# Twenty-two gate groups instead of sixteen, x parked in DRAM, and two linear layers without GpSimd

## The reference

```python
s = jnp.einsum('blhtd,htnd->blhtn', q, sub_keys)
s1, i1 = lax.top_k(s[..., 0, :], 16);  s2, i2 = lax.top_k(s[..., 1, :], 16)
cand = s1[..., :, None] + s2[..., None, :]          # 16 best of 256 a head
...
act = jax.nn.gelu(jnp.einsum('td,tkd->tk', hx, u_tab[ix]))
return jnp.einsum('tk,tkd->td', gx * act, v_tab[ix])
```

## Time and profile before

| what | value |
|---|---|
| runs | 3215.37, 3218.54, 3218.54 us, median 3218.54 us |
| the profiled execution, its own time | 3217.91 us |
| its span, first to last instruction | 3216.1 us |
| mean granted TensorE clock | 0.964 of full speed |
| busy: PE, DVE, ACT, POOL | 2968.4, 2030.7, 1256.4, 155.5 us |

### The profile page before, as it was taken

One profiled execution on the slowest core, in us unless ns is written; L12 is line 12 of the kernel. 1 busy time (PEld: TensorE's weight loads), 2 busy tenths in 40 slices (PEclk: granted clock), 3 DMA queues, 4 the chain that ended last, 5 costly groups with the idle time before them and its releaser, 6 DMA issues. The chain is left out here.

```text
span 3216.1 us, 48665 instructions
## 1 busy us (share of the span) xinstructions
PE 2968.4 (92%) x17528; PEld 2670.5 (83%) x17528; DVE 2030.7 (63%) x3988; ACT 1256.4 (39%) x1826; POOL 155.5 (5%) x116
## 2 busy tenths in 40 slices
PE   7967797899999999999898888978999999999997
PEld 4946697789999999988687787977899999999885
DVE  8867679953348888878735645899534433443454
ACT  3343344753333333333342234458433333333333
POOL 0000350000000000000000012500000000000000
PEclk9988899999999999999988988999999999999999
DMA  5712233574457767767613232336644444444463
GB/s 207 275 39 102 85 118 122 220 246 155 154 183 246 240 237 236 248 193 229 203 46 121 78 119 79 118 125 236 235 153 145 151 155 153 144 152 155 138 176 109
DMA packets 324479, 524.86 MB, mean 163 GB/s; under 512 B 215536, under 2 KB 218352, under 8 KB 319872
## 3 DMA queue, kind: packets, MB, share of 16 engines
q1 hardware_dynamic: 321472, 472.89, 45.4%
q10 hardware_dynamic: 2880, 50.33, 3.9%
HBM read 449.00 MB, written 74.15 MB: 163 GB/s over the span
## 5 line engine op out<-in xcount | busy, mean ns | idle before, releaser
L1952 PE MATMUL pe_s<-peer_hi,pq_uh 128*128 128x384 f32 x2304 | 784.8, 341 | 23.4 <-DVE peer_lo L163 12.6
L163 DVE TENSOR_TENSOR val_vl<-val_vr,val_vh 128x1024 fp32r<-128x1024 f32 x256 | 313.7, 1225 | 757.8 <-ACT val_vh L2115 757.8
L1954 PE MATMUL pe_s<-peer_hi,pq_ul 128*128 128x384 f32 x2304 | 775.9, 337 | 0.0
L1953 PE MATMUL pe_s<-peer_lo,pq_uh 128*128 128x384 f32 x2304 | 775.7, 337 | 0.0
L2052 ACT ACTIVATE pe_A<-pe_s 128x384 f32 (+1 forms) x256 | 126.1, 493 | 1127.2 <-PE pe_s L1954 1127.2
L2019 PE MATMUL peer_acc<-val_vh,val_wh 128*128 128x512 f32 x1536 | 473.2, 389 | 1.0 <-DVE val_wl L163 1.0
L2019 PE MATMUL peer_acc<-val_vh,val_wl 128*128 128x512 f32 x1536 | 474.1, 390 | 0.0
L2019 PE MATMUL peer_acc<-val_vl,val_wh 128*128 128x512 f32 x1536 | 472.9, 389 | 0.0
L1952 PEld LDWEIGHTS pe_s<-peer_hi,pq_uh 128*128 128x128 f32 x2304 | 436.4, 189 | 43.5 <-issue 17.2
L1953 PEld LDWEIGHTS pe_s<-peer_lo,pq_uh 128*128 128x128 f32 x2304 | 436.9, 190 | 8.4
L1954 PEld LDWEIGHTS pe_s<-peer_hi,pq_ul 128*128 128x128 f32 x2304 | 436.4, 189 | 0.0
(11 more groups left out here) (458 smaller groups left out, 3519.6 us busy)
## 6 DMA issues: line engine op xcount, KB each, us to landing
pq_ur<-in_peer_u SPq DMA_DIRECT2D x256, 512.0 KB, 3.7
val_vr<-in_peer_v SPq DMA_DIRECT2D x256, 512.0 KB, 4.5
val_gr<-gates SPq DMA_DIRECT2D x256, 192.0 KB, 4.6
val_mrow<-in_ada_rows SPq DMA_DIRECT2D x56, 512.0 KB, 4.3
gates<-gate_stg ACTq DMA_DIRECT2D x6, 4096.0 KB, 12.5
pq_ur<-in_w_query SPq DMA_DIRECT2D x32, 512.0 KB, 3.6
s_wv<-val_out SPq DMA_DIRECT2D x32, 512.0 KB, 5.2
gates<-gate_stg ACTq DMA_DIRECT2D x4, 3072.0 KB, 13.0
```

The costliest lines, as they stand in the source:

```text
L163: return nc.vector.tensor_tensor(r32(out), x, hi, ALU.subtract)
L1952: pe.matmul(o, r32(uh[:, b, k]), r32(hi[:, k]), start=k == 0, stop=False)
L1953: pe.matmul(o, r32(uh[:, b, k]), r32(lo[:, k]), start=False, stop=False)
L1954: mm = pe.matmul(o, r32(ul[:, b, k]), r32(hi[:, k]), start=False, stop=k == KC - 1)
```

## The change

**Gate groups.** 22 groups of two chunks and a score block, four of them (2, 8, 14 and 20) with three chunks. `LAST` becomes 40, `RING` 44. The order in a group stays: DVE puts `table_low` behind the second chunk, PE runs the score block behind the group's chunks.

**Room.** The ring `A` grows by six blocks. For that, `i1`, `i2`, `gh`, `gl` and `eq` move to the place of `x`. SP stores x (1.57 MB) to DRAM in the query stage and loads it again behind the table, value and gate loads that stand before the slots.

**Rows and builds.** Two of the 24 early rows move from `mix_output` to the end of `mix_input`. In layer 0's slots, rows 0 to 49 stand in slots 34 to 83 as before, and the last six take two slots each (84 to 95), one product in each. Three builds stand in each of slots 34 to 63, two in each of 64 to 83, none in 84 to 95, and two in each of 96 to 126.

**Linear layers.** `Ahead.add` and `Ahead.low_part` go from GpSimd to DVE in both linear layers.

```diff
-IN_ROWS, OUT_ROWS = 2 * KC, KC
+IN_ROWS, OUT_ROWS = 2 * KC + 2, KC - 2
...
+                for i in range(WITH, IN_ROWS):
+                    rows.products(dve, i)
...
-    def low_part(self, pool, b):
-        pool.wait_ge(self.high, b + 1)
-        self.nc.gpsimd.tensor_tensor(r32(self.ul[:, b]), self.ur[:, b], self.uh[:, b], ALU.subtract).then_inc(self.low, 1)
+    def low_part(self, dve, b):
+        dve.wait_ge(self.high, b + 1)
+        lo_part(self.nc, self.ul[:, b], self.ur[:, b], self.uh[:, b]).then_inc(self.low, 1)
...
-        self.nc.gpsimd.tensor_tensor(self.sum[:], a, sq[:, k % self.RING], ALU.add).then_inc(self.added, 1)
+        self.nc.vector.tensor_tensor(self.sum[:], a, sq[:, k % self.RING], ALU.add).then_inc(self.added, 1)
...
-                    rows.products(dve, i)
+                    if i < OUT_ROWS:
+                        rows.products(dve, i)
+                    if i >= 3:
+                        ahead.add(dve, i - 2, sq)
+                    if 4 <= i < 6:
+                        ahead.low_part(dve, i - 4)
...
-GROUP = 3
+GROUPS = [3 if g % 6 == 2 else 2 for g in range(22)]
+SPANS = [range(sum(GROUPS[:g]), sum(GROUPS[:g + 1])) for g in range(22)]
...
-LAST = GATED + CHUNKS // GROUP
+LAST = GATED + len(SPANS)
...
-    THREES, TWOS, LAST_SLOT = ROWS_FROM, ROWS_FROM + 6, ROWS_FROM + 6 + (24 * KC - 18) // 2
+    STARTS = ((0, ROWS_FROM, 3), (90, ROWS_FROM + 30, 2), (130, ROWS_HALF + 12, 2))
...
+            sp.wait_ge(nm.ready, KC)
+            sp.dma_start(d["x_kept"], cx.x[:]).then_inc(xkept, 16)
...
+            sp.wait_ge(gated, CHUNKS)
+            sp.dma_start(cx.x[:], d["x_kept"]).then_inc(xback, 16)
...
-                for u in range(GROUP):
-                    gates((n - GATED) * GROUP + u)
+                for c in SPANS[n - GATED]:
+                    gates(c)
                 late(n)
...
-            for c in range(CHUNKS):
-                one_hots(c)
-                if c % GROUP == 1:
-                    n = GATED + c // GROUP
-                    table_low(n, n % 2)
+            for n in range(GATED, LAST):
+                for c in SPANS[n - GATED]:
+                    one_hots(c)
+                    if c == SPANS[n - GATED][1]:
+                        table_low(n, n % 2)
```

More of the change, by code:

```diff
@@ L689, in mix_input @@
     NY, NV = 18, 8
-    N = NY + NV
+    N, WITH = NY + NV, 2 * KC
     with Stage(nc, sems, "in0") as s:
@@ L729, in _ @@
                         sp.dma_start(d["s5_tab"], tab.all).then_inc(tab.stored, 16)
-                    if i >= N - IN_ROWS + 2:
-                        rows.load(sp, i - (N - IN_ROWS))
+                    if i >= N - WITH + 2:
+                        rows.load(sp, i - (N - WITH))
+                for i in range(WITH, IN_ROWS):
+                    rows.load(sp, i)
                 sp.wait_ge(rstored, 16)
@@ L833, in _ @@
                         dve.sem_inc(chain.made, 1)
-                    if i >= N - IN_ROWS:
-                        rows.products(dve, i - (N - IN_ROWS))
+                    if i >= N - WITH:
+                        rows.products(dve, i - (N - WITH))
+                for i in range(WITH, IN_ROWS):
+                    rows.products(dve, i)
 class Ahead:
@@ L1003, in _ @@
                     square(i)
[L1005 to L1010, removed]
 def scan_output(nc, sems, cx, d, scanned, hi, lo, fin, ahead):
@@ L1067, in _ @@
                         pair(i // 2 - 2)
+                    if i >= 7 and i % 2 == 1:
+                        ahead.add(dve, (i - 5) // 2, sq)
+                    if 9 <= i < 11:
+                        ahead.low_part(dve, i - 9)
                 pair(KC - 2)
+                ahead.add(dve, KC - 2, sq)
                 pair(KC - 1)
@@ L1115, in _ @@
                     ahead.square(act, k, cx.x[:, k], sq)
[L1117 to L1122, removed]
 def rope(nc, sems, cx, d, y, cache):
@@ L1671, with row_slot @@
 ROWS_AHEAD = 2
-ROWS_FROM = 34
+ROWS_FROM, ROWS_HALF = 34, 84
+def row_slot(row):
+    whole = ROWS_HALF - ROWS_FROM
+    return ROWS_FROM + row if row < whole else ROWS_HALF + 2 * (row - whole)
 GATED = FIRST + HOLD
-LAST = GATED + CHUNKS // GROUP
+LAST = GATED + len(SPANS)
 RING = LAST + TAIL
@@ L1740, in slot_of @@
     def slot_of(self, op):
-        return self.THREES + op // 3 if op < 18 else self.TWOS + (op - 18) // 2
+        first, slot, each = [x for x in self.STARTS if x[0] <= op][-1]
+        return slot + (op - first) // each
     def load(self, sp, q):
@@ L1824, in mix_experts @@
     ss = acc[:, 2, 0:T]
-    i1d, i2d, ghd, gld = (s.sb(x, [P, T, 2], F16) for x in ("i1", "i2", "gh", "gl"))
+    (i1d, i2d, ghd, gld), eq = cx.chosen, cx.equal
     warm = s.sb("warm", [P, 1])
@@ L1841, in mix_experts @@
         stg = x.sb("stg", [P, 2, NKEYS, HALF])
-        o1, eq, oh, ol = (x.sb(k, [P, 2, CT, P], F16) for k in ("o1", "eq", "oh", "ol"))
+        o1, oh, ol = (x.sb(k, [P, 2, CT, P], F16) for k in ("o1", "oh", "ol"))
     with Stage(nc, s.sems, f"val{layer}") as x:
@@ L1925, in slot @@
                         sp.dma_start(normg[:], d["norm_g"][:, 2:4]).then_inc(late_loaded, 16)
-                    row = z.n + ROWS_AHEAD - ROWS_FROM
-                    if 0 <= row < LATE_MODS:
+                    for row in (r for r in range(LATE_MODS) if row_slot(r) - ROWS_AHEAD == z.n):
                         if row >= ROWS_AHEAD:
@@ L1933, in _ @@
             slots(sp, slot, looped=layer > 0)
+            sp.wait_ge(xback, 16)
             if layer == 0:
@@ L2356, in _, with modulate @@
             table_low(RING, RING % 2)
-            def modulate(row):
+            def modulate(row, cs):
                 dve.wait_ge(row_loaded[row % ROWS_AHEAD], row // ROWS_AHEAD * 16 + 16)
@@ L2364, in modulate @@
                     dve.wait_ge(silu_loaded, 16)
-                for c, out in ((0, spare[:]), (1, mrow[:, row % ROWS_AHEAD])):
+                for c in cs:
+                    out = mrow[:, row % ROWS_AHEAD] if c else spare[:]
                     ins = v.scalar_tensor_tensor(out, mrow[:, row % ROWS_AHEAD], 1.0, silu[:, c], ALU.mult, ALU.mult,
                                                  accum_out=cx.modT[:, 2 * MODS - LATE_MODS + row, c:c + 1])
-                ins.then_inc(row_used, 1)
+                if c:
+                    ins.then_inc(row_used, 1)
             def modulated():
@@ L2385, in slot @@
                     apply(z, 1)
[L2386 to L2389, removed]
+                    if layer == 0:
+                        for row in range(LATE_MODS):
+                            if z.n < ROWS_HALF and row_slot(row) == z.n:
+                                modulate(row, (0, 1))
+                            elif row_slot(row) >= ROWS_HALF and row_slot(row) in (z.n, z.n - 1):
+                                modulate(row, (z.n - row_slot(row),))
+                        if z.n == row_slot(LATE_MODS - 1) + 2:
+                            modulated()
                     if layer == 0:
@@ L2912, in build @@
     sems = Semaphores(nc)
+    cx = Context()
+    with Stage(nc, sems, "gates") as g:
+        cx.chosen = [g.sb(x, [P, T, 2], F16) for x in ("i1", "i2", "gh", "gl")]
+        cx.equal = g.sb("eq", [P, 2, CT, P], F16)
     with Stage(nc, sems, "g") as g:
-        cx = Context()
-        cx.const, cx.x = g.sb("const", [P, C_KEEP]), g.sb("x", [P, KC, T])
+        cx.x, cx.const = g.sb("x", [P, KC, T]), g.sb("const", [P, C_KEEP])
         cx.modT, cx.scale = g.sb("modT", [P, 2 * MODS, 2]), g.sb("scale", [P, 2, 2, KC, 2])
```

14 lines of the change are left out of this document (10 added, 4 removed).

## The result

The changed kernel takes 3197.72 us (median, 3195.92 to 3201.61), the kernel before, beside it, 3218.54 us. The ratio is 0.9939, 95% interval 0.9923 to 0.9956: faster by 20.8 us, a little under half of the 42.3 forecast. The time lies inside the range given (3160 to 3200), but above the likeliest case's own range, at the time of the second rival (3198).

A forecast was written before the change was run, and what follows sets the result against it. PE was taken to bound the slots and DVE the gate stage and `mix_output`. Slots -50.0, gate stage +13.0, x +3.0 and `mix_output` -8.3 sum to -42.3 us against 3217.9: 3176 us, range 3160 to 3200.

The forecast's parts named there:

- likeliest case: Whole kernel: the forecast as summed, 3176 us, with its own range 3162 to 3190; chance 0.62.
- second rival: Gate stage: all ten stores stall PE 3.2 us each, nothing is caught up, 3198 us; chance 0.15.
- slots: Both layers' slots: six full slots a layer become value slots, saving 24.9 and 25.1 us, together 50.0.
- x back: Before slot 0: loading x from DRAM delays slot 2's gate block, 1.5 us a layer, 3.0 in all, between 0 and 10.
- gate groups: Gate stage: 18 groups of two at 6.0 us and four of three at 8.6 make 142.4, 1.5 over before.
- stores: Gate stage: table loads wait behind gate stores and PE stalls, 5.0 us a layer after catching up, between 0 and 12.
- `mix_output`: First linear layer: two rows fewer and GpSimd quiet, less DVE's added sums and low parts: 8.3 us off, bounds 5 and 9.
- worked-out 7.9: Gate stage: PE's stalls behind five stores a layer, 7.9 us in sum, before the discount to 5.0 for catching up.
- Loads pass the stores: Gate stage: a table load is served beside the store, lands in about 5 us, nobody waits, 3166 us; chance 0.14.
- landing of 11.2 us: Gate stage before the change: a table load issued 2.4 us behind a store's start landed after 11.2 us.
- Every store like the worst: Gate stage: ten stores at 3.2 us of PE stall replace 10.0 us counted, no catching up, 3198 us; chance 0.15.
- ACT the bound: Gate stage: late tables delay evictions and GELU, PE stalls 4.8 to 6.7 us, groups never recover, up to 3233; chance 0.04.

The follow-up runs named there:

- x later: Changed kernel with x loaded back from DRAM at slot 43 instead of before slot 0: 3193.9 us; with each store also cut in four, 3165.8 us.
- stores in pieces: Changed kernel with each 4 MB gate store sent as four of 1 MB, two chunks apart: 3167.6 us, ratio 0.9842 to the kernel before.
- one-key stores: Changed kernel with each gate store writing one key's rows and gates read back from that key, outputs not the reference's: 3163.9 us, ratio 0.9839.
- the halves: Changed kernel with each gate store's four 1 MB parts sent in pairs, four chunks apart: 3165.35 us, ratio 0.9846 to the kernel before.
- GpSimd back: Changed kernel with GpSimd's adds and low parts restored in both linear layers, six rows of products kept: 3200.0 us, ratio 0.995 to the kernel before.
- small packets: Changed kernel with each whole gate store sent as two DMAs in 4 KB runs instead of 32 KB: 3170.2 us, ratio 0.9862 to the kernel before.

## Why the prediction was wrong

Term by term, in the profiled spans (3216.1 us before, 3194.7 after):

| term, both layers | forecast | measured | from |
|---|---|---|---|
| slots | -50.0 | -51.4 | 899.3 and 898.0 to 873.0 twice, x later |
| x back | +3.0 | +1.3 | slots with x earlier and later |
| gate groups | +3.0 | +6.0 | 136.5 to 139.4 and 139.6, stores in pieces |
| stores | +10.0 | +28.9 | spans, whole and in pieces: 3194.7 - 3165.8 |
| `mix_output` | -8.3 | -8.7 | 59.6 to 50.8 |
| the rest | 0 | +2.5 | what is left of the spans' -21.4 |

**The step that failed** is the term of the stores: "The four groups of three leave PE 1.57 us each to catch up, so I take 5.0, between 0 and 12". It measured 28.9 / 2 = 14.5 a layer. Two things were wrong in it above all, the catching up and a price of nothing for the clock behind a stall. Nothing was caught up in layer 0: PE's waits for DVE in front of the third chunk are 6.8 us in 4 with the stalls, and 6.8 in 4 with the stores in pieces. (In layer 1 they are 6.1 and 7.0; there one stall of 1.1 us falls inside a group of three.) The code says why: there are two one-hot buffers, the third chunk's goes where the first's was, and DVE can't begin it before PE has consumed the first. That costs PE 2.41 - 0.87 = 1.5 of the 1.70 us in every group of three, whatever lead DVE has; a lead has nowhere to lie. So the worked-out 7.9 should have stood. The sum before that discount, store by store, was nearer:

| layer 0, store behind chunk | load late for ACT: forecast, measured | PE's stall: forecast, measured |
|---|---|---|
| 7 | 4.8, 5.8 | 1.3, 2.4 |
| 15 | 4.8, 1.3 | 1.3, 0 |
| 23 | 6.7, 8.1 | 3.2, 4.7 |
| 31 | not given, 4.3 | 0.8, 1.0 |
| 39 | 4.8, 6.9 | 1.3, 2.3 |

7.9 became 10.5 (7.8 in layer 1); chunk 15 cost nothing, since a group of three follows it and ACT wants the table later. What no step had was the price behind a stall: 155.0 - 139.4 = 15.6 us in layer 0, of which 10.5 are stalls and 5.1 products at the lower clock; 10.8 in layer 1, of which 7.8 are stalls. (Not all of the other 3.0 in layer 1 is the stores' price: one of its slow spells follows a wait for DVE, shown in the last section, and one such spell makes the stage 1.6 us longer, 141.2 for 139.6, with the one-key stores and the halves too.) Then come 1.3 and 2.0 us in the tail.

How a layer's loss divides between stage and tail differs from run to run. In the two other profiles with 22 groups and whole stores, x later and GpSimd back, the stage of layer 0 takes 152.5 and 152.6 us with 10.9 and 11.0 of stalls, and the tail 24.6. The sum is 177.1 to 177.3 in all three and 160.4 with the stores in pieces: some 16.8 us of loss. In layer 1 the sum is 173.4 to 175.4, against 160.5.

**The groups** were 1.4 us a layer too cheap: a group of three takes 8.81 us as before, not 8.6, and a group of two 6.03: 18 x 6.03 + 4 x 8.81 = 143.8, 2.9 over 140.9.

**The rivals.** "Loads pass the stores" would have given 3166; that is where pieces (3167.6) and small packets (3170.2) put it. The landing of 11.2 us, which the forecast held against it, did not speak for waiting: with turns by packets a load beside a store of large packets lands late as well. "Every store like the worst" gave the measured time, 3198, and was right that nothing is caught up; its 3.2 us a store were wrong for these 22 groups (10.5 / 5 = 2.1), and the clock, which it did not have, made up for it: that it met the time is luck. "ACT the bound" is excluded: groups of two away from the stores take 6.03 us in the changed kernel too.

**Right** were the slots, the three builds, the value slots, `mix_output` to 0.4 us with its parts, and `scan_output` at 0. x was over-sized: its load lands 9.3 us after issue and slot 2 waits, but PE loses only 0.75 and 0.55 us by it.

## What to carry to other kernels

Before a stage is shortened, list what its slack was hiding, work out the lateness event by event, and subtract nothing for catching up unless the trace shows a buffer deep enough to hold the lead. Price a stall of TensorE at more than its length where the granted clock falls behind it. Where a small transfer must not wait behind a large one on another queue, count the packets of both; what helped here was to cut the large one, into pieces spaced over the stage or into packets of the small one's size.

## What the runs showed of the hardware

Two queues took turns by packets, with packets of different size and of the same: 63 and 66 packets in 6.2 us, with 2.06 and 0.27 MB, and 150 and 138 in 2.7 us, with 0.55 and 0.52. So a load of 0.52 MB on SP's queue ended near the end of a store on ACT's queue that was cut into as many packets: 13.7 us for the load and 14.4 for a whole store of 4.19 MB, and 5.7 and 6.0 us where both were issued at 552.6 with a store of 1.05 MB. Alone, such a load takes 3.4 to 3.6.

A load issued 1.3 to 4.3 us into a store (layer 0 of the changed kernel and of the small packets) sent its first packet 4.5 to 4.9 us behind its issue, with large packets and with packets of 4 KB alike; alone, or issued within 0.1 us of a 1.05 MB store, 1.0 us behind.

The granted clock did not follow the length of a stall alone. In layer 1 of the changed kernel it fell behind a wait of 1.9 us for DVE (the first row) and stayed up through a stall of 2.65 us (the second and third):

```profile
2130.00:2135.00 5.00, 3.08 (x21) 3.09 (x22) 5.00 (x10) 4.56 (x3) 0.00 (x0) 0.71 0.34 105
...
2230.00:2235.00 5.00, 3.79 (x33) 3.45 (x31) 3.20 (x6) 1.59 (x2) 0.00 (x0) 1.00 0.36 147
2235.00:2240.00 5.00, 3.56 (x31) 3.60 (x32) 5.00 (x9) 5.00 (x5) 0.00 (x0) 1.00 0.33 108
```

What decides between the two was not tried.
